# Two blocks of two layers on one core: ends of stages joined, scales from narrow sums, products begun on parts

## The reference

```
# first block, layer i: a mixer, then 32 experts (4 groups of 8), of which each token uses 2
x = layer_norm(ALPHA * x + y_mixer @ w_o[i], ln1_g[i], ln1_b[i])
for g in range(4):          # all 8 experts of a group on all tokens, weighted by combine (mostly 0)
    h = silu(einsum('td,edf->tef', x, w_gate[g])) * einsum('td,edf->tef', x, w_up[g])
    out += einsum('tef,efd->td', h * combine[:, g, :, None], w_down[g])
x = layer_norm(ALPHA * x + out, ln2_g[i], ln2_b[i])

# second block, layer l
h = rmsnorm(x, attn_norm[l]);  proj = h @ w_in[l]          # three branches: nsa, differences, sgu
p = softmax(q k);  o = (p[:, :, 0] - lam * p[:, :, 1]) @ v  # differences of 4 heads of width 128
o_b = rmsnorm(o, diff_subln) * (1 - lambda_init)            # over a head's 128 values
gates = sigmoid(h @ w_merge[l] + b_merge[l])
mixed = gates[0] * (o_a @ w_branch_a) + gates[1] * (o_b @ w_branch_b) + gates[2] * (o_c @ w_branch_c)
x = x + mixed @ w_out[l]
h = rmsnorm(x, ffn_norm[l])
x = x + (silu(h @ w_ffn1[l]) * (h @ w_ffn3[l])) @ w_ffn2[l]
```

## Time and profile before

| | us |
|---|---|
| median of 3 runs | 2245.68 (2244.87 to 2246.35) |
| the profiled execution's own time | 2248.68 |
| its span | 2246.9 |
| PE busy / DVE busy / ACT busy | 2098.1 (93%) / 1110.8 (49%) / 748.4 (33%) |
| mean granted TensorE clock | 0.971 of full speed |

### The profile page before, as it was taken

The page is one execution under the profiler, slowest core; times in us unless marked ns, Lnnn a source line. Parts: engine busy times, 40 slices in busy tenths (PEclk is TensorE's granted clock), DMA queues, the critical chain, the costliest instruction groups (busy, mean ns, idle before and its releaser), DMA issues.

```text
span 2246.9 us, 30715 instructions
## 1 busy us (share of the span) xinstructions
PE 2098.1 (93%) x13024; PEld 1515.2 (67%) x13024; DVE 1110.8 (49%) x1893; ACT 748.4 (33%) x1376; POOL 62.7 (3%) x96
## 2 busy tenths in 40 slices
PE   7989999998979899999999799999999999999998
PEld 7974443443468734334343689999997889999996
DVE  5864232222266622222222676666554585765554
ACT  4751111010135411011000554543443455444442
POOL 3000000000000000000000000010000000010000
PEclk9999999999989999999999899999999999999999
DMA  8628999999973499999999524454554623454552
GB/s 266 213 102 361 427 426 427 427 428 428 423 255 150 188 383 428 427 427 427 427 427 415 199 78 146 142 193 141 182 188 175 210 76 127 151 189 159 188 188 75
DMA packets 130256, 600.35 MB, mean 267 GB/s; under 512 B 6028, under 2 KB 26640, under 8 KB 103744
## 3 DMA queue, kind: packets, MB, share of 16 engines
q1 hardware_dynamic: 125808, 590.37, 66.6%
q10 hardware_dynamic: 3072, 6.74, 0.8%
q0 software_dynamic: 1232, 1.19, 0.4%
HBM read 597.22 MB, written 1.05 MB: 266 GB/s over the span
## 4 chain that ended last, share of the span: by engine, by line
PE 73%; DMA 16%; DVE 6%; ACT 3%; issue 1%; SPq 1%; DVEq 0%; ACTq 0%
PE ps L1579 13%; PE ps L454 9%; PE ps L455 9%; PE ps L456 9%; DMA ring<-in_w_up 8%; DMA rx<-in_w_up 8%; PE ps L1619 6%; PE ps L471 2%; PE ps L473 2%; PE ps L472 2%; PE ps L554 2%; PE ps L2959 2%; PE ps L949 2%; PE ps L2961 2%; PE ps L2960 2%; PE ps L1508 1%
## 5 line engine op out<-in xcount | busy, mean ns | idle before, releaser
L430 DVE TENSOR_TENSOR CL<-ring,CH 128x1024 fp32r<-128x1024 f32 x284 | 333.5, 1213 | 254.2 <-ACT CH L425 253.5
L454 PE MATMUL ps<-XTH,CH 128*128 128x256 f32 x1456 | 418.3, 287 | 0.0
L455 PE MATMUL ps<-XTL,CH 128*128 128x256 f32 x1456 | 412.3, 283 | 0.0
L456 PE MATMUL ps<-XTH,CL 128*128 128x256 f32 x1456 | 412.2, 283 | 0.0
L1579 PE MATMUL ps<-ring,ARM 128*64 128x512 f32 x1024 | 356.7, 612 | 31.2 <-DMA ring<-in_w_up 22.5
L1579 PE MATMUL ps<-rx,ARM 128*64 128x512 f32 x1024 | 357.0, 612 | 19.2 <-DMA rx<-in_w_up 12.0
L425 ACT ACTIVATE CH<-ring 128x1024 fp32r<-128x1024 f32 x284 | 283.3, 1045 | 137.6 <-PE ps L2961 60.8
L454 PEld LDWEIGHTS ps<-XTH,CH 128*128 128x128 f32 x1456 | 279.8, 192 | 2.9 <-issue 2.5
L455 PEld LDWEIGHTS ps<-XTL,CH 128*128 128x128 f32 x1456 | 280.0, 192 | 0.4
L456 PEld LDWEIGHTS ps<-XTH,CL 128*128 128x128 f32 x1456 | 279.7, 192 | 0.0
L1579 PEld LDWEIGHTS ps<-ring,ARM 128*64 128x64 f32 x1024 | 115.2, 141 | 189.5 <-issue 142.2
(11 more groups left out here) (428 smaller groups left out, 3672.9 us busy)
## 6 DMA issues: line engine op xcount, KB each, us to landing
rx<-in_w_gate SPq DMA_DIRECT2D x32, 2048.0 KB, 23.4
ring<-in_w_gate SPq DMA_DIRECT2D x32, 2048.0 KB, 24.2
ring<-in_w_down SPq DMA_DIRECT2D x32, 2048.0 KB, 27.2
ring<-in_w_ffn SPq DMA_DIRECT2D x30, 2048.0 KB, 8.2
ring<-in_w_up SPq DMA_DIRECT2D x28, 2048.0 KB, 26.4
rx<-in_w_down SPq DMA_DIRECT2D x28, 2048.0 KB, 26.8
rx<-in_w_up SPq DMA_DIRECT2D x28, 2048.0 KB, 27.8
ring<-in_w_in SPq DMA_DIRECT2D x14, 2048.0 KB, 8.5
```

Source lines behind the costliest of these rows:

```text
L430: v.e.tensor_tensor(pc.lo[:, cs], pc.ap[:, cs], pc.hi[:, cs].bitcast(F), ALU.subtract).then_inc(dve_done, v.put("lo", pc.k, q))
L454: p.e.matmul(o, pc.hi[:, c, n0:n0 + 128], src[0][:, c, :], start=c == 0, stop=False)
L455: p.e.matmul(o, pc.hi[:, c, n0:n0 + 128], src[1][:, c, :], start=False, stop=False)
L456: m = p.e.matmul(o, pc.lo[:, c, n0:n0 + 128], src[0][:, c, :], start=False, stop=c == nk - 1)
```

## The change

1. The load list is made of halves of units. In the experts, the two experts' halves alternate; the last units come in the order gate 14, up 14, gate 15, up 15, down 14, down 15, where down 14 stood before gate 15. The down matrices of pairs 14 and 15 come in halves, up 15 whole.
2. PE's end of the experts: the up products of pairs 14 and 15 come before either down product, and `pe_last_down` makes these by halves of c: 14 first half, 14 second half, back of 14 (n = 0), 15 first half, back of 14 (n = 1), 15 second half, back of 15. Pair 15 gets a hidden tile and banks of its own. DVE and ACT follow.
3. The waits of `over_ready` stand inside the `If`.
4. `load_gb` moves from pair 4 to behind the last down half's landing.
5. The first norm of the second block (`dve_begin`) of t = 0 runs between the two halves of the last layer norm of t = 1.
6. The differences' scales: 8 matmuls of one column with the squares as stationary operand give the sums in 8 columns; root and reciprocal are taken there, DVE multiplies the identity by them (128x1024), and two matmuls of 512 columns with ones bring the scales to all rows. One DVE operation for 256 columns takes the place of four reciprocals, products and scalings. Four sigmoids come before the root on ACT.
7. The output product of n = 0 does chunks 0 to 4 of both t, then 5 to 7. Both folds stand behind the last output product, in layer 0's feed-forward part too.
8. The feed-forward part's down products wait for each chunk of `fh` instead of the last; the last chunks of t = 0 are in another order.

The diff, cut to its core:

```diff
-            loads.append(u)
+            loads.extend((u, h) for h in range(u.halves))
...
+                MU = [[None] * 3 for _ in range(16)]
+                order = [(pair, q) for pair in range(14) for q in range(3)]
+                order += [(14, 0), (14, 1), (15, 0), (15, 1), (14, 2), (15, 2)]
+                for n, (pair, q) in enumerate(order):
+                    us = []
+                    for x in range(2):
+                        e = (l, (2 * pair + x) // 8, (2 * pair + x) % 8)
+                        if q < 2:
+                            src = major(I[("w_gate", "w_up")[q]][e], 0, 512), 8, 512
+                        else:
+                            src = I["w_down"][e].rearrange("(p c) n -> p c n", p=128), 4, 1024
+                        u = Unit(*src, slots[0], 2 if n == 4 or n > 45 else 1)
+                        if slots[0] in extra:
+                            u.after = (l, extra.index(slots[0]))
+                        slots.append(slots.pop(0))
+                        u.freed = [(0, ("moe", l, pair, q, h)) for h in range(2)]
+                        us.append(u)
+                    loads.extend((u, h) for h in range(us[0].halves) for u in us)
+                    MU[pair][q] = us
...
+            if between:
+                between(0)
...
+        def pe_down_part(l, pair, b, n, c, ht):
+            us = moes[l].units[pair][2]
+            p.wait_ge(dve_done, v.at("turn", l, pair))
+            for x in range(2):
+                landed(p, us[x], c // 2)
+                i = p.e.matmul(b[64 * x:64 * x + 64, :], ht[:, c, 64 * x:64 * x + 64],
+                               us[x].ap[:, c, n * 512:n * 512 + 512], start=c == 0, stop=c == 3)
+            i.then_inc(pe_done, p.put("down", l, pair, n, c))
+        def pe_last_down(l):
+            m = moes[l]
+            bs = [[take(("down", l, pair, n), i) for n, i in enumerate(ii)] for pair, ii in ((14, (B_Y0, B_Y1)), (15, (B_G, B_U)))]
+            for pair, ht in ((14, m.HT), (15, m.HT2)):
+                for h in range(2):
+                    if pair == 15:
+                        pe_back(l, 14, h)
+                    for n in range(2):
+                        for c in (2 * h, 2 * h + 1):
+                            pe_down_part(l, pair, bs[pair - 14][n], n, c, ht)
+                        if h:
+                            p.name("down", l, pair, n)
+                    p.name("moe", l, pair, 2, h)
...
-                pe_down(l, pair, (lambda: pe_back(l, 15, 0)) if pair == 15 else None)
+                if pair < 14:
+                    pe_down(l, pair)
+            pe_last_down(l)
+            pe_back(l, 15, 0)
...
-                if pair == 4:
-                    act_gb(l)
                 if pair == 14:
                     some = over_flag(a, l)
+            act_down(l, 14)
+            act_gb(l)
+            act_down(l, 15)
...
             some = over_flag(v, l)
+            dve_down(l, 14)
+            dve_back(l, 14, 0)
+            dve_back(l, 14, 1)
             dve_down(l, 15, (0,))
+            dve_down(l, 15, (1,))
             dve_back(l, 15, 0)
-            dve_down(l, 15, (1,))
-            dve_back_stats(0)
+            dve_back_stats(0, 0)
+            dve_back_stats(1, 0)
             dve_back(l, 15, 1)
-            dve_back_stats(1)
+            for t in range(2):
+                dve_back_stats(t, 1)
...
             for t in range(2):
-                v_layer_norm(f"ln2 {l}", t, 32 * (2 * l + 2), 2, X)
+                v_layer_norm(f"ln2 {l}", t, 32 * (2 * l + 2), 2, X, dve_begin if l and t else None)
...
         def pe_over(l, some):
             o, m = overs[l], moes[l]
-            over_ready(p, l)
             if p.known is None:
                 return
             e = p.e
             with e.If(some > 0):
+                over_ready(e, l)
...
         def pe_sums(l):
             d = diffs[l]
-            for k in range(2):
-                b = take(("dsum", l, k))
-                p.wait_ge(act_done, a.at("dsq", l))
-                p.e.matmul(b, C("ones"), d.SQ[:, 512 * k:512 * k + 512], start=True,
-                           stop=True).then_inc(pe_done, p.put("dsum", l, k))
+            b = take(("dsum", l))
+            p.wait_ge(act_done, a.at("dsq", l))
+            for k in range(8):
+                i = p.e.matmul(b[:, k:k + 1], d.SQ[:, 128 * k:128 * k + 128], C("ones")[:, 0:1], start=True, stop=True)
+            i.then_inc(pe_done, p.put("dsum", l))
+        def pe_scales(l, k):
+            d = diffs[l]
+            b = take(("dscale", l, k))
+            p.wait_ge(dve_done, v.at("ddiag", l))
+            p.e.matmul(b, C("ones"), d.SQ[:, 512 * k:512 * k + 512], start=True,
+                       stop=True).then_inc(pe_done, p.put("dscale", l, k))
...
+            r = small("dsums", 8)
+            a.wait_ge(dve_done, v.at("dsum", l))
+            a.e.activation(r, r, ACT.Sqrt).then_inc(act_done, a.put("dsd", l))
...
+            c = 0.2 + 0.6 * math.exp(-0.3 * l)
+            v.wait_ge(pe_done, p.at("dsum", l))
+            v.e.tensor_scalar(small("dsums", 8), tile("dsum", l)[:, 0:8], 1.0 / (128 * c * c), 1e-6 / (c * c), ALU.mult,
+                              ALU.add).then_inc(dve_done, v.put("dsum", l))
+        def dve_scales(l):
+            d, r = diffs[l], small("dsums", 8)
+            v.wait_ge(act_done, a.at("dsd", l))
+            v.e.reciprocal(r, r).then_inc(dve_done, v.put())
+            v.own()
+            v.e.tensor_tensor(d.SQ.rearrange("p (k t) -> p k t", k=8), bc_mid(C("ident"), 8), bc_end(r, 128),
+                              ALU.mult).then_inc(dve_done, v.put("ddiag", l))
...
-        def dve_difference(l, k, second):
+        def dve_difference(l, k):
             d = diffs[l]
             q = slice(256 * k, 256 * k + 256)
-            if not second:
-                v.wait_ge(act_done, a.at("dsd", l))
-                v.own()
-                v.e.reciprocal(d.R[:, q], d.R[:, q]).then_inc(dve_done, v.put())
-                return
             hi, lo = o_part(l, 1, k)
-            v.own()
-            v.e.tensor_tensor(d.R[:, q], d.O.rearrange("p j t -> p (j t)")[:, q], d.R[:, q],
-                              ALU.mult).then_inc(dve_done, v.put())
-            v.own()
-            v.e.tensor_scalar(d.R[:, q], d.R[:, q], VT[:, 66 + l:67 + l], 0.2 + 0.6 * math.exp(-0.3 * l), ALU.mult,
-                              ALU.mult).then_inc(dve_done, v.put())
+            v.wait_ge(pe_done, p.at("dscale", l, k // 2))
+            v.e.scalar_tensor_tensor(d.R[:, q], d.O.rearrange("p j t -> p (j t)")[:, q], VT[:, 66 + l:67 + l],
+                                     tile("dscale", l, k // 2)[:, 256 * (k % 2):256 * (k % 2) + 256], ALU.mult,
+                                     ALU.mult).then_inc(dve_done, v.put("dscale", l, k // 2))
...
+                    if n == 1 and j < 2:
+                        pe_scales(l, j)
...
+            for t in range(2):
+                p_toks(("wout", l, 0, t), p_piece(f, PIECE[6][0]), t, ms_, list(range(5)), lambda c: (f"mixed{l}", c),
+                       last=False)
             for n, t in WO_ORDER:
-                p_toks(("wout", l, n, t), p_piece(f, PIECE[6][n]), t, ms_, list(range(8)),
-                       lambda c: (f"mixed{l}", c))
-                if (n, t) == (2, 1):
-                    p_folded(f"merge norm{l}", 0)
-            p_folded(f"merge norm{l}", 1)
+                p_toks(("wout", l, n, t), p_piece(f, PIECE[6][n]), t, ms_, list(range(0 if n else 5, 8)),
+                       lambda c: (f"mixed{l}", c), first=n > 0)
+            for t in range(2):
+                p_folded(f"merge norm{l}", t)
...
-                        act_roots(l)
+                        a_warm(ACT.Sigmoid)
...
+                if n == 0:
+                    act_roots(l)
...
+                        if (n, j) == (0, 1):
+                            dve_scales(l)
+                        elif (n, j) == (0, 3):
+                            dve_sgu_normed(l)
...
-            p.wait_ge(dve_done, v.at("fh", l, 21))
             def down(i, t, n):
                 pc = p_piece(f, W_DOWN + i)
                     hi, lo = (x[:, 2 * i + c, t * 128:t * 128 + 128] for x in w.H)
                     wh, wl = (x[:, c, n * 512:n * 512 + 512] for x in (pc.hi, pc.lo))
                     p_half(pc, c)
+                    p.wait_ge(dve_done, v.at("fh", l, 2 * i + c))
...
-                for n in range(2):
-                    down(9, t, n)
-                    down(10, t, n)
-                    if l == 0 and (t, n) == (1, 0):
-                        p_folded("ffn norm0", 0)
+                for i, n in ((9, 0), (9, 1), (10, 0), (10, 1)) if t == 0 else ((9, 0), (10, 0), (9, 1), (10, 1)):
+                    down(i, t, n)
             if l == 0:
-                p_folded("ffn norm0", 1)
+                for t in range(2):
+                    p_folded("ffn norm0", t)
...
         def act_gb(l):
             a.wait_ge(dve_done, v.at("tokens", l))
```

(3 more changed lines are left out.)

135 lines of the change are left out of this document (55 added, 80 removed).

## The result

| | before | changed |
|---|---|---|
| median, us | 2246.01 (4 runs, 2244.87 to 2246.36) | 2213.77 (4 runs, 2211.54 to 2215.68) |
| profiled execution: own time / span | 2248.68 / 2246.9 | 2211.54 / 2209.7 |
| mean granted clock | 0.971 | 0.982 |

The ratio is 0.9857, with a 95% interval of [0.984, 0.9874]; in a later series of five runs it was 0.9847 [0.9833, 0.986]. That is 32 to 34 us less; 2211.5 was forecast.

A forecast was written before the change was run, and what follows sets the result against it. Transfers were taken to bound the experts' middle, PE's waits and lower clock to cost time in the second block. Eight terms sum to 34.2 us off 2248.7; the median, 3.0 lower, is 2211.5 us, range 2202 to 2223.

The forecast's parts named there:

- 4, scales: Second block, differences' sums: PE's 3.57 us wait and 2.9 lost to clock go, narrow products cost 1.9; 9.2 us in all.
- 5, output product on parts: Second block's output product: PE's 1.5 us wait for MXL goes behind chunks of the other t; 3.0 us in two layers.
- 6, merge's folds: Second block's merge: with both folds behind the last product, the second's wait and clock loss go; 6.6 us in all.
- 7, down products: Feed-forward part: the first down products need chunk 0 alone, so waits on FL and most on CL go; 5.0 us in all.
- 8, layer 0's last folds: Behind layer 0's feed-forward part: 3.3 us of waits and about 0.9 of clock loss go; 4.2 us, once.
- Term 1: Experts' loads: gamma and beta leave the saturated stream, 2.45 us less per layer, 4.9 us in all.
- Term 2: Experts' end: chain ends 0.6 us earlier, but a gap ahead of up 15 may drop the clock; 1.0 us lost in all.
- Term 3: Starts behind the norms: 1.7 us earlier at the second block's start, 0.6 behind layer 0; 2.3 us in all.
- Rival C: Norm behind the experts: gamma and beta land late, 4.3 us twice, giving 2220 us; chance 0.10.
- D: Differences' scales, second block: the wait at the sums stays or moves to the scales, giving 2221 us; chance 0.12.
- B: Experts' tail: the gap drops the clock and it stays low, 22.3 us more per layer, giving 2256 us; chance 0.04.
- E: More comes: no clock drop in the experts' tail, cheap narrow columns, clock kept up elsewhere, giving 2204 us; chance 0.14.

The follow-up runs named there:

- oldsums: Changed kernel with the differences' scales as before (wide sums, root and reciprocals on 1024 columns, roots ahead of the sigmoids): 2220.08 us, ratio to before 0.9891.
- oldparts: Changed kernel with the output product of n = 0 in one piece per t and down products waiting for the last fh: 2218.95 us, ratio to before 0.9883.
- oldfolds: Changed kernel with the first fold ahead of the last product again, in both merges and behind layer 0's feed-forward part: 2223.73 us, ratio to before 0.9905.
- gb4: Changed kernel with gamma and beta asked for at pair 4 again, amid the experts' loads: 2216.7 us, ratio to before 0.9872.
- gbonly: Kernel before with only late gamma and beta, asked for when the last down half has landed: 2246.04 us, ratio to before 1.0000.
- oldtail: Changed kernel with the experts' end as before (load order, products, adds and statistics), gamma and beta still late: 2217.74 us, ratio to before 0.9882.
- tailonly: Kernel before with only the experts' new end (load order, halves, products, adds' order), gamma and beta early: 2244.78 us, ratio to before 0.9995.
- Rootslate: Changed kernel with wide sums, root and four reciprocals on 1024 columns, but ACT's changed order (sigmoids before roots): 2218.37 us, ratio to before 0.9873.
- after2: Changed kernel run again in a later series, no edit: 2212.6 us, ratio to before 0.9847.

## Why the prediction came true, and where it was off

**The sum.** 34.2 us were forecast and 32.2 to 33.8 measured. The second block's mechanisms are shown one by one; in the first block larger errors cancel, and that the sum came so near is in part luck. The second block's terms, in us:

| term | forecast | measured, by what |
|---|---|---|
| 4, scales | 4.6 per layer | 4.9 and 3.9 (oldsums); 4.9 and 4.8 from before to after |
| 5, output product on parts | 1.5 per layer | 1.8 (oldparts) |
| 6, merge's folds | 3.3 per layer | 3.0 and 3.4 (oldfolds) |
| 7, down products | 2.5 per layer | 1.6 (oldparts), all of it for FL: the CL waits are gone in oldparts too, so their part (1.0 at the end of layer 1) comes from the order of the last chunks, which no run isolated |
| 8, layer 0's last folds | 4.2 | 6.1 (oldfolds), with a stretch at 0.50 between the folds that before doesn't have |

Term 6's rival within it (the first fold waits in its turn) did not come: no wait on DR is left. Narrow products: 1.70 us where 1.9 was forecast, so a row of 64 columns priced one column well, and 16 passes took 0.106 us each. The Trainium skill, "TensorE: Matmul & The Clock Gate", section "LDWEIGHTS (loading the stationary operand)", has a load take its columns / 1.2 ns, 107 ns for 128: the trace agrees with that, and not with the issue floor that I had weighed, and each pass has a load of its own in it (16 loads for the 16 passes).

**Terms 1 and 2, the experts.** Term 1's mechanism and size hold: 2.45 forecast, 2.7 by gb4 and 2.9 by gbonly in layer 1's stage. Term 2 is read best from the landing of the last down half to the end of the statistics: 12.7 us in both layers of the three kernels with the old end (before, gbonly, oldtail), 12.8 to 12.9 with the new one (changed, gb4, tailonly). So the new end costs 0.1 to 0.2 us per layer, where I took 0.5, but not as I reasoned. The step that failed is "the gap is nearest to the row of 2.72": PE waited 1.22 us for up 15, not 2.9, and no level was lost (1.00 in all three stretches). The 0.6 us that I had for that case were used up by the chain from up 15's landing to the statistics' end: 32.8 us (597.54 to 630.36) instead of 31.7, each product and back 0.1 to 0.25 us longer than I took.

Some 2 us more in layer 1 were in no term. After the first up product of layer 1, the last half lands 447.4 us in before and 444.6 in gbonly, but 442.5 in oldtail and 442.4 to 443.2 in the changed kernel and those that keep its experts; with early gamma and beta it is 445.0 in tailonly and 445.5 in gb4. Oldtail has the old order of products, so this gain is not the new end's. What sets it, no run isolates; the load list made of halves is one thing that these kernels share and that before and gbonly lack. In layer 0 the one profile of before is late besides: its last half lands at 623.35, that of gbonly at 617.1, and 2.45 of this are the bytes.

By the medians, each of the two parts alone gave nothing measurable, and both together, with the starts, the first block's 3 to 4 us. I had priced them as independent. For late gamma and beta alone the trace gives the reason, the request's place behind the evictions; whether it needs the new end at all is not shown.

**Term 3.** 1.7 forecast at the second block's start, 1.5 measured. Behind layer 0, 0.6 forecast and 0.3 measured.

**Rival C.** Its condition, a wait of the norm for gamma and beta, did not hold here: they landed 8.4 us after their issue at most, where I had estimated 8, and 16.9 was the row of the saturated stream. (The rival's own sum has a slip: 641 less 636.3 is 4.7, not 4.3, which makes it 1 us dearer.) The engines were still full, and between 622 and 625 the two queues show what I had counted on, packets one for one, and two thirds of the bytes for gamma and beta:

```profile
q10 hardware_dynamic: 212, 0.80, 66.6%
q1 hardware_dynamic: 211, 0.41, 35.8%
```

The weights' packets are of 2 KB here, and of 15 KB in the earlier trace rows, where the counts were near equal as well. The first packet for gamma started at 621.2, 3.7 us after its request. No run changed the packet size with all else the same.

**Rivals D, B and E.** D's wait for the scales did not come in the changed kernel, but its margin was smaller than I took: the scales' products started 10.4 us behind the sums, not some 20, and the chain took 6.9, so 3.5 us were left. Rootslate shows that it would have, in another form, had the reciprocals stayed wide. B did not come. E's conditions partly held (no drop in the tail, and some 2 us more in layer 1's stream), and yet the total was not lower, for the reason that follows.

**What the prediction had not.** The moba mixer became 4.3 us longer, with no instruction changed. Here are the stretches behind its two waits of 2.0 us on DVE, first in before (columns as in the earlier trace rows):

```profile
733.20:736.40 3.20, 1.96 (x16) 1.32 (x16) 1.44 (x5) 1.12 (x2) 0.00 (x0) 1.00 0.01 3
737.20:740.70 3.50, 3.44 (x28) 2.37 (x29) 1.63 (x5) 2.75 (x5) 0.00 (x0) 1.00 0.02 5
```

And of the changed kernel:

```profile
728.00:731.20 3.20, 3.19 (x16) 2.32 (x16) 0.39 (x2) 1.19 (x2) 0.00 (x0) 0.51 0.01 3
733.40:736.60 3.20, 3.17 (x20) 2.12 (x22) 0.77 (x3) 2.47 (x4) 0.00 (x0) 0.73 0.03 5
735.00:738.50 3.50, 3.50 (x18) 1.88 (x15) 1.36 (x4) 3.47 (x5) 0.00 (x0) 0.53 0.02 5
```

In before, PE runs at 1.00 behind both; in after at 0.51 behind the first, which ends at 728.0, and partly at the lower level behind the second, which ends at 733.4, with the same waits of 2.01 us. From the end of the first wait to that of the second it is 5.4 us instead of 4.0, and from there to the next long wait 39.7 instead of 38.1: that is 3 us; the rest is in the mixer's first 10 us (0.84 against 0.77) and last. The lower level behind the first wait stands in every one of the ten profiles whose kernel has the new end and at least one of late gamma and beta and the new starts (the mixer takes 139.3 to 142.0 us), and in none of the four others (before, gbonly, tailonly, oldtail; 135.2 to 137.9). Behind the second it stands in nine of the ten, not in after2. The two waits are 4.0 us together in all fourteen. What sets the level there stays open: the mixer's starts overlap in the two groups (641.0 to 650.0 against 642.4 to 647.4).

From the end of layer 0's statistics to that of layer 1's it takes 608.0 us in before and 607.5 in after: there the loss in the mixer has eaten nearly all that the starts and the experts of layer 1 gained. Tailonly, without the loss, has 604.4.

## What to carry to other kernels

A chain of small operations that frees a bank or writes a scale should lie beside other work of the waiting engine. In the second block, PE's waits behind its first fold fell from 25 us to under 2, and the block became 29.5 us shorter, since each wait of over 2 us had 0.3 to 2.9 us of lower clock behind it, which goes with it. Where a request is issued from the queue of an engine that also computes, look at what stands ahead of it there: gamma and beta asked for at the last landing were in time, and behind two evictions, 6.7 us later, they were waited for. A change of order that takes a wait off one engine needs a look at the next queue: without cheaper work on DVE, 3.4 us were waited there.

## What the runs showed of the hardware

- A product of 128 rows by 1 column costs TensorE 1.70 / 16 = 0.11 us per pass, hardly less than one of 64 columns (0.12).
- The float32 fold against a diagonal took 0.24 to 0.25 us per pass at either level: 32 passes in 7.80 us at the changed kernel's first merge, at 1.00 throughout, and 32 in 7.88 at the second block's start, of which the first 5.5 us have 0.50. The lower clock costs nothing there. The transposes of the norm's rows, passes of 128 columns too, do follow the clock: 8 in 1.97 us at 0.50 and 16 in 1.93 at 1.00.
- Behind PE's last product in the experts, where only a skipped branch lies between, the next product could start 5.55 us later in layer 0 and 5.8 in layer 1, in both kernels with products on constants, though no wait shows in the profile. That the branch itself takes this time is the likely reading, and no run took it out.
- Equal waits of 2.0 us were followed by the upper level in four profiles and by the lower in ten others, and constants kept one stretch up only to lose another.
- A small load on a second queue beside a saturated one went packet for packet: 86 to 88 beside packets of 15 KB, and 212 to 211 beside packets of 2 KB; it landed after up to 16.9 and 8.4 us.
